# Where a two-block transformer kernel makes the first two weight sums of its seven-product matmuls

## The reference, cut to what matters

```
h = rmsnorm(x)
f = square(relu(h @ w_ff1)) @ w_ff2        # w_ff1: 2048 x 8192, w_ff2: 8192 x 2048
```

## Time and profile before

| What | us |
|---|---|
| Median of 3 runs | 2220.96 (2220.9 to 2222.22) |
| Span of the profiled execution, first to last instruction | 2219.3 |
| TensorE matmul busy | 2195.5 (99%) |
| VectorE busy | 1613.8 (73%) |
| ScalarE busy | 1163.2 (52%) |
| GpSimd busy | 93.2 (4%) |
| Moved by DMA | 402.65 MB, 181 GB/s |

### The profile page before, as it was taken

How to read it: one execution, slowest core, us unless ns; L and a number is a source line. 1 busy time by engine, 2 the same in 40 slices (tenths; PEclk the granted TensorE clock), 3 DMA queues, 4 the chain that set the end, 5 groups by cost and what they waited for, 6 DMA issues and landing times.

```text
span 2219.3 us, 32872 instructions
## 1 busy us (share of the span) xinstructions
PE 2195.5 (99%) x13128; PEld 1892.6 (85%) x13128; DVE 1613.8 (73%) x2013; ACT 1163.2 (52%) x1682; POOL 93.2 (4%) x66
## 2 busy tenths in 40 slices
PE   8999999999999999999999999999999999999998
PEld 7888988888888888888898988888888888888886
DVE  7878565665454599899886578847454547998997
ACT  6433465543443466566664466646434345665665
POOL 0553000000000000000000000000000000000000
PEclk9999999999999999999999999999999999999999
DMA  8364445555556666667654533455565565666663
GB/s 328 121 153 161 151 134 211 168 190 189 189 188 188 187 194 207 195 205 258 199 166 144 172 115 98 136 196 163 187 189 189 189 189 173 215 201 195 209 202 114
DMA packets 169923, 402.65 MB, mean 181 GB/s; under 512 B 15296, under 2 KB 30912, under 8 KB 165968
## 3 DMA queue, kind: packets, MB, share of 16 engines
q1 hardware_dynamic: 158496, 394.83, 55.3%
q10 hardware_dynamic: 11312, 6.22, 1.2%
HBM read 398.90 MB, written 2.13 MB: 181 GB/s over the span
## 4 chain that ended last, share of the span: by engine, by line
PE 94%; DVE 4%; ACT 1%; issue 1%; DMA 0%; SPq 0%; DVEq 0%; ACTq 0%
PE ps L768 21%; PE ps L773 11%; PE ps L841 7%; PE ps L842 6%; PE ps L843 6%; PE ps L657 5%; PE ps L857 3%; PE ps L856 3%; PE ps L858 3%; PE ps L665 3%; PE ps L666 3%; PE ps L667 3%; PE ps L1075 2%; PE ps L1077 2%; PE ps L1076 2%; PE ps L679 2%
## 5 line engine op out<-in xcount | busy, mean ns | idle before, releaser
L2497 DVE TENSOR_TENSOR w_low<-raw_weights,w_high 128x1024 fp32r<-128x1024 f32 (+1 forms) x403 | 474.3, 1215 | 422.1 <-ACT w_high L1574 418.3
L1574 ACT ACTIVATE w_high<-raw_weights 128x1024 fp32r<-128x1024 f32 (+1 forms) x378 | 377.4, 1046 | 408.0 <-PE ps L773 279.8
L768 PE MATMUL ps<-x_split,w_high 128*128 128x512 f32 x2048 | 494.1, 391 | 1.7 <-DVE x_split L2485 1.7
L768 PEld LDWEIGHTS ps<-x_split,w_high 128*128 128x128 f32 x2048 | 374.6, 188 | 74.2 <-issue 3.0
L773 PEld LDWEIGHTS ps<-x_split,w_low 128*128 128x128 f32 x2048 | 265.8, 191 | 12.1
L773 PE MATMUL ps<-x_split,w_low 128*128 128x256 f32 x2048 | 269.4, 283 | 0.0
L841 PE MATMUL ps<-w_high,x_split 128*128 128x512 f32 x672 | 262.0, 390 | 0.5 <-issue 0.4
L842 PE MATMUL ps<-w_low,x_split 128*128 128x512 f32 x672 | 261.5, 389 | 0.0
L843 PE MATMUL ps<-w_high,x_split 128*128 128x512 f32 x672 | 261.4, 389 | 0.0
L2582 DVE TENSOR_TENSOR w_low<-raw_weights,w_high 128x1024 fp32r<-128x1024 f32 x168 | 197.8, 1219 | 1.7 <-ACT w_high L1689 1.6
L1689 ACT ACTIVATE w_high<-raw_weights 128x1024 fp32r<-128x1024 f32 x168 | 167.6, 1045 | 0.0
(11 more groups left out here) (376 smaller groups left out, 3657.9 us busy)
## 6 DMA issues: line engine op xcount, KB each, us to landing
raw_weights<-in_w_ff SPq DMA_DIRECT2D x128, 1024.0 KB, 5.4
raw_weights<-in_w_up SPq DMA_DIRECT2D x64, 1024.0 KB, 5.2
raw_weights<-in_w_down SPq DMA_DIRECT2D x64, 1024.0 KB, 5.5
raw_weights<-in_w_in SPq DMA_DIRECT2D x62, 1024.0 KB, 5.3
raw_weights<-in_w_out SPq DMA_DIRECT2D x32, 1024.0 KB, 4.9
raw_weights<-in_w_mem_kv SPq DMA_DIRECT2D x7, 1024.0 KB, 14.6
residual<-in_xT SPq DMA_DIRECT2D x2, 2048.0 KB, 13.9
region<-t_table ACTq DMA_DIRECT2D x1, 3072.0 KB, 18.9
```

The lines of the kernel that those rows point to most:

```text
L768: nc.tensor.matmul(hidden_ps(g)[:, c], w[:, P * c:P * c + P], xs[:, kt], start=(kt == 0), stop=False, skip_group_check=True)
L1574: nc.scalar.activation(split_slot(wh_t, k)[:, r], ring_slot(n)[:, r], ACT.Copy).then_inc(rounded, 1)
L2497: V.tensor_tensor(split_slot(wl_t, k)[:, r], ring_slot(n)[:, r], split_slot(wh_t, k)[:, r].bitcast(f32), ALU.subtract).then_inc(split_read ...
```

## The change

SUMMED becomes the even slots from 2 to 28, 14 a pass. The sums t1 and t3 of the summed slots are no longer made in the downs. In iterations 1 to 7 of the ups, after the splits of every second slot, VectorE makes those of one summed slot of the down that follows (`staged_sums`, 28 in each up). POOL loads that slot's weights for it (1 MB, `load`) into an idle tile, `mixed` in block 1 and `residual` in block 2, and stores the sums to the DRAM tensor `weight_sums` (512 KB, `store`); one semaphore, `staged`, counts both. POOL issues the load of record c + 1 and then the store of record c when sum c is made. VectorE waits, before sum c, for load c and store c - 1.

In the downs SP loads record c (512 KB) into `rinv`: record 0 with slot 4, and each later one with the slot four places behind the previous summed slot, just ahead of that slot's own load. VectorE's and ACT's readers wait for it (`raws_loaded`). VectorE makes the sums of the first slot of a pass at r = 1 and no longer at r = 0, in both passes. `first_product` and `combine` move one slot later.

```diff
@@ -160,6 +160,7 @@
         ps = ctx.enter_context(nc.psum_tensor("ps", [P, 8, 512], f32))
+        w_sums = nc.dram_tensor("weight_sums", (28, P, 2048), f32, kind="Internal").ap()
@@ -208,7 +209,8 @@
         sums_x = {n: (t[:, 0:896], t[:, 896:1792]) for n, t in (("ff2_1", mixh_t), ("ff2_2", xres_over))}
-        sums_at = [(rinv, place("sums", 22528, 1024)), (region[:, 16384:17408], region[:, 17408:18432])]
+        sums_a, sums_b = rinv, place("sums", 22528, 1024)
+        stage_of = {"ff1_1": mix_t, "ff1_2": xres_t, "ff2_1": mix_t, "ff2_2": xres_t}
@@ -273,6 +275,8 @@
         out_written = sem("out_written")
+        staged, sums_staged = sem("staged"), sem("sums_staged")
+        rest_loaded, raws_loaded = [sem(f"rest{i}_loaded") for i in range(2)], sem("raw_sums_loaded")
@@ -456,7 +460,11 @@
         PAIRS = FT // 2
-        SUMMED = (2, 5, 7, 10, 12, 15, 17, 20, 22, 25, 27)
+        SUMMED = tuple(range(2, PAIRS - 3, 2))
+        RECORDS = 2 * len(SUMMED)
+        STAGED = 4
+        STAGE0 = {"ff1_1": 0, "ff1_2": RECORDS, "ff2_1": 0, "ff2_2": RECORDS}
+        ADDS = 1
@@ -477,10 +485,6 @@
             return hid_f[:, 512 * r + a:512 * r + a + width]
-        def scratch_of(h, r):
...
-            return sums_at[1 if (h, r) == (0, SUMMED[0]) else 0]
@@ -535,17 +539,22 @@
             def down(name, w):
-                for j in range(BODY):
-                    load(rows(w, 0, 1024, 2 * j, 2))
                 n0, k0 = SLOT0[name], SPLIT0[name]
-                for lo, hi, back, c0 in ((1, FF2_ITERS // 2, 0, 0), (FF2_ITERS // 2, FF2_ITERS, DFF, 1024)):
-                    with sp.Fori(lo, hi) as i:
-                        for j in range(BODY):
-                            sp.wait_ge(split_ready, i * (2 * BODY) + 2 * (k0 + j - RING + 1))
-                            src = w[bass.ds(i * (2 * BODY * P) + (2 * P * j - back), 2 * P), c0:c0 + 1024]
-                            sp.dma_start(ring_slot(n0 + j).rearrange("p (k c) -> p k c", k=2),
-                                         src.rearrange("(k p) c -> p k c", p=P)).then_inc(slot_loaded[(n0 + j) % RING], 16)
-                state["n"] = n0 + BODY * FF2_ITERS
+                before = {}
+                for c in range(RECORDS):
+                    before[4 if c == 0 else slot_before(c - 1, SUMMED) + 4] = c
+                for q in range(2 * PAIRS):
+                    (h, r), n = divmod(q, PAIRS), n0 + q
+                    sp.wait_ge(split_ready, 2 * (k0 + q - RING + 1))
+                    if q == 4:
+                        sp.wait_ge(staged, 32 * (STAGE0[name] + RECORDS))
+                        sp.wait_ge(split_used, k0)
+                    if q in before:
+                        c = before[q]
+                        sp.dma_start(sums_a, w_sums[c, :, 0:1024]).then_inc(raws_loaded, 16)
+                    src = w[2 * P * r:2 * P * (r + 1), 1024 * h:1024 * h + 1024].rearrange("(k p) c -> p k c", p=P)
+                    sp.dma_start(ring_slot(n).rearrange("p (k c) -> p k c", k=2), src).then_inc(slot_loaded[n % RING], 16)
+                state["n"] = n0 + 2 * PAIRS
@@ -1692,7 +1701,6 @@
                 s, w = SUMMED0[name] + c, ring_slot(n)
-                sums_a, sums_b = scratch_of(h, r)
@@ -1700,16 +1708,18 @@
                     act.wait_ge(split_used, SPLIT0[name])
+                    act.wait_ge(staged, 32 * (STAGE0[name] + RECORDS))
...
                 act.wait_ge(slot_loaded[n % RING], 16 * (n // RING + 1))
-                act.wait_ge(sums_made, 6 * s + 6)
+                act.wait_ge(sums_made, 5 * s + 5)
...
                 nc.scalar.activation(sh[:, 384:896], sums_b[:, 512:1024], ACT.Copy).then_inc(sums_rounded, 1)
+                act.wait_ge(raws_loaded, 16 * (s + 1))
@@ -1735,7 +1745,7 @@
                             home_done(r - (PAIRS - 4))
-                        if r == PAIRS - 3:
+                        if r == PAIRS - 2:
@@ -2240,9 +2250,30 @@
                 m.did(nc.gpsimd.tensor_tensor(sq[:, a], sq[:, a], sq[:, a + 1], ALU.add), name, "gathered", c)
+            def stage(name, w, free):
...
+                t = stage_of[name]
...
+                def store(c):
+                    pool.wait_ge(sums_staged, ADDS * (STAGE0[name] + c + 1))
+                    if c + 1 < RECORDS:
+                        load(c + 1)
+                    pool.dma_start(w_sums[c, :, 0:1024], t[:, 2048:3072]).then_inc(staged, 16)
...
+                def load(c):
+                    h, r = c // len(SUMMED), SUMMED[c % len(SUMMED)]
+                    src = w[2 * P * r:2 * P * (r + 1), 1024 * h:1024 * h + 1024].rearrange("(k p) c -> p k c", p=P)
+                    pool.dma_start(t[:, 0:2048].rearrange("p (k c) -> p k c", k=2), src).then_inc(staged, 16)
...
+                free()
+                load(0)
+                for c in range(RECORDS):
+                    store(c)
...
             gather("outn", 0, near_sq, 0)
+            stage("ff1_1", A["w_ff2"], lambda: pool.wait_ge(dve_done, at("t5_masked")))
@@ -2250,6 +2281,7 @@
             gather("window", 1, xo, 8)
+            stage("ff1_2", A["w_down_2"], lambda: pool.wait_ge(act_done, at("residual_row", 1)))
@@ -2543,9 +2575,19 @@
                     V.scalar_tensor_tensor(h, h, 0.0, h, ALU.max, ALU.mult).then_inc(hidden_ready, 1)
+                t = stage_of[name]
+                w, sums_ = (t[:, a:a + 2048].rearrange("p (b c) -> p b c", c=512) for a in (0, 2048))
...
+                def staged_sums(q, i):
+                    c = STAGE0[name] + q - STAGED
+                    dve.wait_ge(staged, i * (32 * STAGED) + (32 * c + 16))
+                    V.tensor_tensor(sums_[:, 0:2], w[:, 1:3], w[:, 0].unsqueeze(1).to_broadcast([P, 2, 512]), ALU.add).then_inc(sums_staged, 1)
...
                         low(name, j, i)
+                        if j % 2 == 0 and not first:
+                            staged_sums(j // 2, i)
@@ -2583,36 +2625,30 @@
                 def sums(h, r):
-                    n, s = SLOT0[name] + PAIRS * h + r, SUMMED0[name] + summed_count(h, r)
-                    (sums_a, sums_b), w = scratch_of(h, r), ring_slot(n).rearrange("p (b c) -> p b c", c=512)
-                    t1, t2, t13 = sums_a[:, 0:512], sums_b[:, 0:512], sums_a.rearrange("p (b c) -> p b c", c=512)
+                    n, s, c = SLOT0[name] + PAIRS * h + r, SUMMED0[name] + summed_count(h, r), summed_count(h, r)
...
                         dve.wait_ge(hidden_ready, HIDDEN_OF[name] + r // 2 + 1)
-                    if (h, r) == (0, SUMMED[0]):
-                        dve.wait_ge(t5_out, 16)
-                    elif (h, r) == (0, SUMMED[1]):
-                        dve.wait_ge(split_used, SPLIT0[name])
-                    c = summed_count(h, r)
...
                         dve.wait_ge(split_ready, 2 * (SPLIT0[name] + slot_before(c - 1, SUMMED) + 1))
+                    else:
+                        dve.wait_ge(split_used, SPLIT0[name])
                     V.tensor_tensor(s13, x[:, 0:2], x[:, 2::-2], ALU.subtract).then_inc(sums_made, 1)
+                    dve.wait_ge(raws_loaded, 16 * (s + 1))
                     dve.wait_ge(slot_loaded[n % RING], 16 * (n // RING + 1))
-                    V.tensor_tensor(t13, w[:, 1:3], w[:, 0].unsqueeze(1).to_broadcast([P, 2, 512]), ALU.add).then_inc(sums_made, 1)
-                    dve.wait_ge(sums_made, 6 * s + 1)
+                    w, t1, t2 = ring_slot(n).rearrange("p (b c) -> p b c", c=512), sums_a[:, 0:512], sums_b[:, 0:512]
+                    V.tensor_tensor(t2, w[:, 2], t1, ALU.add).then_inc(sums_made, 1)
+                    dve.wait_ge(sums_made, 5 * s + 1)
                     V.tensor_tensor(s2, s1, x[:, 1], ALU.subtract).then_inc(sums_made, 1)
-                    dve.wait_ge(sums_made, 6 * s + 2)
-                    V.tensor_tensor(t2, w[:, 2], t1, ALU.add).then_inc(sums_made, 1)
-                    dve.wait_ge(sums_made, 6 * s + 3)
+                    dve.wait_ge(sums_made, 5 * s + 2)
+                    V.tensor_tensor(w[:, 0], w[:, 3], t2, ALU.add).then_inc(sums_made, 1)
+                    dve.wait_ge(sums_made, 5 * s + 3)
                     V.tensor_tensor(s4, x[:, 3], s2, ALU.add).then_inc(sums_made, 1)
-                    dve.wait_ge(sums_made, 6 * s + 4)
-                    V.tensor_tensor(w[:, 0], w[:, 3], t2, ALU.add).then_inc(sums_made, 1)
...
                     n, k, s = SLOT0[name] + PAIRS * h + r, SPLIT0[name] + PAIRS * h + r, SUMMED0[name] + summed_count(h, r)
-                    sums_a, sums_b = scratch_of(h, r)
@@ -2629,16 +2665,14 @@
                             home_done(r - (PAIRS - 3))
-                        if r == PAIRS - 2:
+                        if r == PAIRS - 1:
...
                                 ahead(t)
-                        if r == 0:
-                            sums(h, SUMMED[0])
-                            if h:
-                                keep(name, 0)
-                        elif r + 1 in SUMMED[1:]:
+                        if (h, r) == (1, 0):
```

(2 more changed lines are left out.)

## The result

The changed kernel takes **2424.03 us** (median of 4 runs, 2423.04 to 2430.36) against 2221.34 us (2220.9 to 2222.22) before: ratio 1.0916, 95% interval 1.0901 to 1.0932. It is 9.2% slower. The forecast was 2389 us with a range of 2350 to 2450. The profiled execution is the longest of the four (2430.36 us), 6.3 us above their median, so lengths read from it are a little high.

The account below looks back on a forecast made before the run. TensorE, busy 99% of the span, was taken as the bound. Terms: 2219.3 us span - 8.2 (fewer matmuls) + 166.4 (record waits) + 6 (down starts) + 4 (ups) = 2387.5, plus 1.7 to the median: 2389 us, range 2350 to 2450.

Parts of the forecast that it names:

- The mechanism: Downs: each record's load stands in VectorE's program with plain(r) queued behind; 3.5 us wait, 52 times, TensorE idle, +166 us.
- I take 3.6 us: Downs: assumed landing time of a record's 512 KB load, giving a VectorE wait of 3.5 us per record.
- VectorE's own part: Downs: VectorE's work in a pair of slots, 11.08 - 1.13 = 9.95 us, against 10.2 us of TensorE.
- my ends of 2.7 and 5.4: Downs: lower and upper end, in us, given for the landing of a record's 512 KB load.
- The wake-up: Downs: 0.06 us counted in the 3.85 us from VectorE's last end to the sum that needs the record.
- Start of each down ... +6 us: Start of downs: record 0 lands late and sums(0, 2) waits behind last_summed; about 3 us a down, +6 us.
- the 3.2 of a pair: Downs: TensorE's idle time per pair of slots, VectorE taking 13.4 us where TensorE needs 10.2.
- I take +4 us: Ups: cost of the staging's loads and stores beside the ring's, +4 us for both, ends 0 and +52.
- Rival 1: The ups become bound by DMA, at 329 GB/s: 2389 + 48 = 2437 us; chance 0.17.
- Rival 3: Downs: TensorE's clock falls after idle gaps, plain slots at half clock, 117 us more, 2506 us; chance 0.05.
- the prediction's bound of 14: Downs: below 14 slow matmuls a pair, TensorE's idle 3.2 us absorbs them all.

Follow-up runs that it names:

- e6: The changed kernel with a second place for the loaded records in pass 1 of each down only: 2336.85 us, ratio 1.0524.
- e7: The changed kernel with a second place for the loaded records in both passes of each down: 2241.46 us, ratio 1.0085.
- e3: The changed kernel with only 32 KB of 512 loaded of each record but the first of a down: 2306.07 us, ratio 1.0381.
- e5: The changed kernel with two places for the staged sums in the ups and separate counters for loads and stores: 2419.04 us, ratio 1.0893.
- e8: The changed kernel with the edits of e7 and e5 together: 2238.86 us, ratio 1.0078.
- e11: e9 with the first record loaded 2 us earlier still and ACT's first rounding waiting for one sum less: 2228.29 us, ratio 1.0031.
- e10: e9 with VectorE's sums reordered so that ACT may begin rounding earlier: 2238.3 us, ratio 1.0077.
- e9: e8 with each down's first record loaded at the end of the up and its sums made ahead of last_summed: 2231.15 us, ratio 1.0043.

## Why the prediction was right, and where its sizes were off

*The mechanism.* Right in each of its parts: the wait's place, its count, what is queued behind it and who waits for it. e6 and e7 give it back by one more buffer, e3 in part by a shorter load. Against the median the sum was 35 us short, against the profiled span 41 (+168 us for +209); the terms below are those of the profile.

*"I take 3.6 us" for the record's landing.* This term was too small. It landed in 4.2 us, so the wait is 3.76 us and not 3.45. A pair takes 13.84 us over the four passes and not 13.4: for the 48 pairs measured that is 21 us of the 41, some 14 of the longer wait and 7 of VectorE's own part, 10.1 us where the prediction had 9.95. The landing lay inside my ends of 2.7 and 5.4; taking the value just below the 576-KB row (3.7 us), which had no other load around it, was the weak choice. One record, in pass 2 of the first down, takes 6.8 us beside the read of the t5 table; its 3 us are in the 21. The wake-up that the sum took as 0.06 us is 0.02 in this trace. The rule of the Trainium skill ("DMA: Bandwidth & Descriptors", Anatomy of one DMA), 2.0 us plus bytes over 436 GB/s, gives 3.2 us here; the page fits it to DMAs issued by GpSimd, and this one is SP's. The trace does not agree with it: 512 KB take 4.2 us and 1 MB 7.0 where the rule has 4.4, and the measured rows decide.

*"Start of each down ... +6 us".* Slot 1 was 3.6 us late for 3 expected; the gap before slot 3 was 4.8 us, 1.6 more than the 3.2 of a pair; and at the change of pass, which I had priced at nothing, 1.4 us go. That is 3.6 us more in the first down and much the same in the second, 7 in all.

*"I take +4 us" for the ups.* They cost 13.3 us in this profile, 9 more; by the medians e5 gives back 5 of them. I had seen that VectorE waits for load c and store c - 1, and priced only the bandwidth. The chain through the store was the term left out, and e5 shows it: same bytes, ups 0.9 and 0.0 us longer. Rival 1 named the right place and the wrong mechanism: the DMA share is 0.92, but TensorE is full at 0.94 as well. The traffic still counts through the landing times: ring loads take 7.0 us in the median for 5.4 before, and the stores 8.9.

*Rival 3, the clock.* It did fall, and its sign, matmuls more than 0.23 us apart inside the slots, is there; the price of the rival, 117 us, is not. Windows of 1 us in the kernel after, behind an idle stretch of TensorE from 843.3 to 846.3 us; the number behind the engines is the granted clock.

```profile
844.00:845.00 1.00, 0.00 (x0) 0.00 (x0) 1.00 (x2) 1.00 (x2) 0.00 (x0) 1.00 0.00 0
846.00:847.00 1.00, 0.68 (x2) 0.62 (x3) 1.00 (x3) 1.00 (x2) 0.00 (x0) 0.62 0.00 0
848.00:849.00 1.00, 1.00 (x3) 0.73 (x3) 1.00 (x2) 1.00 (x2) 0.00 (x0) 0.50 0.75 213
852.00:853.00 1.00, 1.00 (x6) 0.81 (x6) 0.00 (x0) 0.00 (x0) 0.00 (x0) 1.00 0.59 172
```

After the idle 3 us the engine runs at 0.50 of full speed (1.2 GHz) for some microseconds. In every other pair (26 of 52) 7 to 14 matmuls of the plain slot come 0.43 us apart instead of 0.23. The Trainium skill ("TensorE: Matmul & The Clock Gate", HAM oscillation) warns of this, and the trace agrees that it happens. It costs nothing where VectorE sets the pair: a slot with such matmuls ends later and the gap behind it is shorter by as much, as the prediction's bound of 14 said. In the plain slot of 970.23 us 13 matmuls are 0.43 us apart, the summed slot behind it begins at 978.47, and the next plain slot starts only 0.61 us after that one's last matmul starts; behind the plain slot of 956.63, which has none of these, it is 3.55 us. In the pairs VectorE waits for no result of TensorE. Where TensorE was the bound the same clock did cost time: 1.7 us at the start of e8's first down, about 5 us in the ups here, and 2.3 us in the slot of 2172.38, which has 11 such matmuls and only plain slots behind the next.

*The rest.* Of the 41 us some 21 + 7 + 9 = 37 are placed; the slot of 2172.38 (2.3 us) and the wait before the last slot of the second down (1.3 more than before) are nearly all of the other 4.

## What to carry to other kernels

When a result moves from being computed in place to being loaded, the question is which instruction frees its buffer and which one needs the next: if they are neighbours on one engine, the whole landing stands in that engine's program, and a second place (183 us, e7) was worth more than a sixteenth of the bytes (118 us, e3). Check a new chain (load, compute, store, next) by its sum of latencies, and the longest of them, and not only by its bytes. And an engine at 97% of the pair has no room left for handovers: even with every planned wait gone (e11), the 8.2 us that TensorE saved, and 5 us more, went to gaps in the downs, the longest 0.8 to 2.0 us.

## What was not expected of the hardware

- A VectorE instruction that waits for the one right before it starts 0.11 to 0.12 us later than one that doesn't (e10 and e9: 0.72 against 0.61, 0.32 against 0.20). The Trainium skill ("VectorE: DVE Perf Modes", The DRAIN you can't avoid) says of eight tensor_copy in a row that a semaphore after each costs nothing extra; these rows, of tensor_tensor, differ from it.
- 32 KB behind other traffic landed in 1.8 us, less than the 2 KB of the earlier trace rows in 2.4.
- Two queues together moved 318 GB/s at a DMA share of 0.94 through a whole up and delayed TensorE by less than a microsecond (e5).
